# Stick-breaking attention: scores from high and low parts, and the projections that feed them one half-step earlier

## What is computed

```python
def stick_breaking_attention(h, w_qkv, w_o):
    qkv = (h @ w_qkv).reshape(b, s, 3, SB_HEADS, HEAD_DIM)
    q, k, v = qkv[:, :, 0], qkv[:, :, 1], qkv[:, :, 2]
    ...
        z = jnp.einsum('bqhd,bshd->bhqs', q_blk, k).astype(jnp.float32) * scale
        causal = key_pos[None, :] < t[:, None]
        log_1m = jnp.where(causal, jax.nn.log_sigmoid(-z), 0.0)
        excl = lax.cumsum(log_1m, axis=3, reverse=True) - log_1m
        a = jnp.where(causal, jnp.exp(jax.nn.log_sigmoid(z) + excl), 0.0)
        return jnp.einsum('bhqs,bshd->bqhd', a.astype(v.dtype), v)
```

## Times and profile before

| | us |
|---|---|
| median of 3 runs | 2158.74 |
| lowest, highest | 2157.59, 2158.87 |
| the profiled execution, device time | 2157.02 |
| its span, first to last instruction | 2155.2 |

### The profile page before, as it was taken

How to read it: one execution, slowest core, us unless ns; L and a number is a source line. 1 busy time by engine, 2 the same in 40 slices (tenths; PEclk the granted TensorE clock), 3 DMA queues, 4 the chain that set the end, 5 groups by cost and what they waited for, 6 DMA issues and landing times.

```text
span 2155.2 us, 32285 instructions
## 1 busy us (share of the span) xinstructions
PE 2120.9 (98%) x12608; PEld 1768.3 (82%) x12608; DVE 1536.7 (71%) x2132; ACT 1002.8 (47%) x1690; POOL 727.5 (34%) x604
## 2 busy tenths in 40 slices
PE   8999999999999999999999999999999999999998
PEld 6888788888999998766688999988965568898987
DVE  5866566557988876387759787776567756777774
ACT  4433464345544444465554333344536755343434
POOL 2300330017434434074554332311146636332321
PEclk9999999999999999999999999999999999999999
DMA  5233125313333333311133333233420012323231
GB/s 178 83 108 88 50 78 159 86 57 91 99 109 108 112 94 98 88 40 50 40 88 99 99 98 118 85 112 101 142 66 2 1 40 79 118 88 108 93 104 49
DMA packets 293303, 188.77 MB, mean 88 GB/s; under 512 B 8224, under 2 KB 287008, under 8 KB 293152
## 3 DMA queue, kind: packets, MB, share of 16 engines
q1 hardware_dynamic: 292864, 186.51, 28.9%
q10 hardware_dynamic: 288, 0.21, 0.0%
HBM read 183.81 MB, written 2.10 MB: 86 GB/s over the span
## 4 chain that ended last, share of the span: by engine, by line
PE 89%; DVE 5%; ACT 3%; issue 2%; POOL 0%; DMA 0%; ACTq 0%; DVEq 0%; POOLq 0%
PE ps L539 87%; PE ps L573 2%; DVE wl L512 1%; ACT wh L502 1%; DVE sb_small L3228 1%; DVE H L682 0%; DVE tmp L1169 0%; ACT XH L560 0%; ACT sq L616 0%; DVE ns_x L3268 0%; DVE ns_x L3267 0%; ACT p_xscr L722 0%; DVE nt_pts L3251 0%; DMA p_xt<-in_x 0%; ACT tp_tb L1894 0%
## 5 line engine op out<-in xcount | busy, mean ns | idle before, releaser
L512 DVE TENSOR_TENSOR wl<-raw,wh 128x1024 fp32r<-128x1024 f32 (+1 forms) x336 | 433.1, 1302 | 239.7 <-ACT wh L502 239.2
L539 PE MATMUL ps<-xb_x,wh 128*128 128x256 f32 (+1 forms) x1584 | 388.6, 336 | 2.2 <-DVE wl L512 1.0
L502 ACT CAST wh<-raw 128x1024 fp32r<-128x1024 f32 (+1 forms) x336 | 324.3, 980 | 132.6 <-PE ps L539 123.8
L539 PEld LDWEIGHTS ps<-xb_x,wh 128*128 128x128 f32 x1584 | 265.2, 188 | 32.1 <-ACT tp_q L2104 0.9
L539 PE MATMUL ps<-tt_t,wh 128*128 128x256 f32 x1536 | 277.5, 280 | 2.0 <-ACT tp_q L2100 2.0
L539 PE MATMUL ps<-xb_x,wl 128*128 128x256 f32 (+1 forms) x792 | 264.8, 334 | 0.0
L539 PEld LDWEIGHTS ps<-tt_t,wh 128*128 128x128 f32 x1536 | 237.1, 188 | 5.8 <-ACT tp_q L2100 2.9
L539 PE MATMUL ps<-XH,wh 128*128 128x512 f32 (+2 forms) x632 | 234.5, 371 | 4.9 <-issue 4.0
L539 PE MATMUL ps<-XH,wl 128*128 128x512 f32 (+2 forms) x632 | 229.8, 364 | 0.0
L539 PE MATMUL ps<-XL,wh 128*128 128x512 f32 (+2 forms) x632 | 229.4, 363 | 0.0
L539 PE MATMUL ps<-tt_t,wl 128*128 128x256 f32 x768 | 214.2, 279 | 0.0
(11 more groups left out here) (429 smaller groups left out, 4669.9 us busy)
## 6 DMA issues: line engine op xcount, KB each, us to landing
raw<-in_mlp_w SPq DMA_DIRECT2D x128, 512.0 KB, 4.0
raw<-in_w_gate_up SPq DMA_DIRECT2D x44, 512.0 KB, 3.9
raw<-in_w_in SPq DMA_DIRECT2D x29, 512.0 KB, 3.7
raw<-in_sb_w_qkv SPq DMA_DIRECT2D x24, 512.0 KB, 3.6
raw<-in_w_down SPq DMA_DIRECT2D x22, 512.0 KB, 5.9
raw<-in_w_out_mix SPq DMA_DIRECT2D x16, 512.0 KB, 3.5
raw<-in_w_kv SPq DMA_DIRECT2D x16, 512.0 KB, 3.7
raw<-in_nsa_w_kv SPq DMA_DIRECT2D x12, 512.0 KB, 3.6
```

The lines of the kernel that those rows point to most:

```text
L502: e.copy(shaped(WH[i % NH], i), source(i)).then_inc(*w_hi.up(i))
L512: e.tensor_tensor(shaped(WL[i % NH], i), source(i), shaped(WH[i % NH], i).bitcast(F), ALU.subtract).then_inc(*w_lo.up(i))
L539: return e.matmul(out, a, b, start=start, stop=stop, skip_group_check=True)
```

## The change

Queries and keys are now split. `dve_stick_qk` evicts a projection in float32 into one of two `tmp` buffers instead of into `q_s` or `k_s`. A new ACT cast, `act_stick_qk`, writes the high part (fp32r) to `q_s` or `k_s`. A new DVE subtraction, `dve_stick_qk_lo`, writes the low part to one of four buffers (`qk_lo`, tiles `sl_a`, `sl_b`, `sl_c`). `pe_stick_scores` makes three fp32r products for each head (high by high, low queries, low keys), first for both heads, then the next, and waits for the low parts. `next_qk` is one step ahead of what it was, so that the loops run from n = -2: a projection is made in steps (0,1), (2,3), ... instead of (1,2), (3,4), ...; its eviction and both new steps stand in even n, the weight cast on ACT in even n and the weight subtraction on DVE in odd n (before: odd and even).

```diff
--- before.py
+++ after.py
@@ -2272,12 +2272,16 @@
 
 
     ph = Phase(XAT, "st")
-    q_s = ph.sb("q", [128, 8, S])
-    k_s = ph.sb("k", [128, 8, S])
+    q_s = ph.sb("q", [128, 8, S], R)
+    k_s = ph.sb("k", [128, 8, S], R)
     XO = Pair(*(Phase(XAT + 4 * 8 * S * i, f"so{i}").sb("x", [128, 8, S], R) for i in range(2)))
     ph = Phase(PH0 + 32768, "st")
     v_s = ph.sb("v", [128, 4, D])
     rs1 = Phase(PH0 + 92160, "st").sb("rs1", [128, S])
+    phl = Phase(PH0 + 94208, "sl")
+    qk_lo = [[Phase(PH0 + 90112, "sl").sb("a", [128, S], R), phl.sb("b", [128, S], R)],
+             [phl.sb(f"c{i}", [128, S], R) for i in range(2)]]
+    qk_low = [[Buf(t) for t in pair] for pair in qk_lo]
     wd = [512 - 128 * j for j in range(4)]
     wl_ = [512, 384, 384, 128]
     ST = [(c, j) for c in range(8) for j in (3, 2, 1, 0)]
@@ -2311,26 +2315,43 @@
 
     def next_qk(n):
 
-        u, half = (n + 1) // 2 + 2, (n + 1) % 2
+        u, half = (n + 2) // 2 + 2, n % 2
         return (u if u < 16 else None), half
+
+    def left_qk(n):
+
+        u, half = next_qk(n - 1)
+        return QK[u] if half and u is not None and n > -2 else None
 
     OUT_AT = {NST - 2: [(0, 0, 2)], NST - 1: [(0, 2, 6)], NST: [(0, 6, 7), (1, 0, 2)], NST + 1: [(1, 2, 6)],
               NST + 2: [(1, 6, 7)]}
     OUT_LAST = [(2, 0, 3), (0, 7, 8), (1, 7, 8), (2, 3, 8)]
 
     def plan_stick():
+        def plan_qk(o, bank):
+            plan(bank, ("sqk", o), (v_made, ("sqk", o)))
+
+        def plan_parts(u):
+            o = QK[u]
+            plan(tmp.bufs[2 + u % 2], ("qkt", o), (x_lo, ("qk", o)))
+            plan(qk_low[o % 8 % 2][o // 8], ("qkl", o), (scored, ("z", 4 * (o % 8) + 3, 1)))
+
         for o in QK[0:2]:
-            plan(psr.next(), ("sqk", o), (v_made, ("sqk", o)))
+            plan_qk(o, psr.next())
         for blk in range(2):
             token_plan(f"sv{blk}", 4)
             if blk == 0:
                 plan_spread("st")
+        for u in range(2):
+            plan_parts(u)
         plan_spread("one")
+        for u in range(2, 16):
+            plan_parts(u)
         pairs = Ring([0, 1, 2])
-        for n in range(-1, NST):
+        for n in range(-2, NST):
             u, half = next_qk(n)
             if u is not None and half == 0:
-                plan(NB, ("sqk", QK[u]), (v_made, ("sqk", QK[u])))
+                plan_qk(QK[u], NB)
             if n < 0:
                 continue
             c, j = ST[n]
@@ -2392,12 +2413,15 @@
     def pe_stick_scores(e, n):
 
         c, j = ST[n]
-        e.wait_ge(*v_made.at("sqk", c))
-        e.wait_ge(*v_made.at("sqk", 8 + c))
+        e.wait_ge(*x_lo.at("qk", c))
+        e.wait_ge(*x_lo.at("qk", 8 + c))
         bk = [take(e, ("sk", n, m))[:, 0:wd[j]] for m in range(2)]
-        for m in range(2):
-            p0 = 64 * m
-            mm(e, bk[m], k_s[p0:p0 + 64, c, 128 * j:128 * j + 128], q_s[p0:p0 + 64, c, 128 * j:512], True, False)
+        ql, kl = got(("qkl", c)), got(("qkl", 8 + c))
+        for k, q, first in ((k_s[:, c, :], q_s[:, c, :], True), (k_s[:, c, :], ql, False),
+                            (kl, q_s[:, c, :], False)):
+            for m in range(2):
+                p = slice(64 * m, 64 * m + 64)
+                mm(e, bk[m], k[p, 128 * j:128 * j + 128], q[p, 128 * j:512], first, False)
         for m in range(2):
             mm(e, bk[m][:, 0:128], Ib[:, :], maskb[:, 2, :], False, False).then_inc(*scored.up("z", n, m))
 
@@ -2460,6 +2484,7 @@
             pe_tokens(e, f"sv{blk}", [f"sv{blk}{c}" for c in range(4)], XB, "st", 512, 4, 2,
                       between={0: pe_sum, 2: pe_spread} if blk == 0 else {})
         pe_spread(e, "one")
+        pe_stick_qk(e, -2)
         pe_stick_qk(e, -1)
         for n in range(NST + 3):
             if n < NST:
@@ -2479,6 +2504,10 @@
             project(e, f"so{o}", XO, "so", t[:, :], ("soo", o))
         pe_.end("st")
 
+    def act_stick_qk(e, o):
+        e.wait_ge(*v_made.at("sqk", o))
+        e.copy((k_s if o >= 8 else q_s)[:, o % 8, :], got(("qkt", o))[:, :]).then_inc(*x_hi.up("qk", o))
+
     def act_stick(e):
         act_weights(e, UI["sv02"])
         fence(e, "f")
@@ -2494,6 +2523,9 @@
                 act_weights(e, UI[f"sv{blk}{c}"] + 2)
                 if blk == 0 and c == 2:
                     act_rs(e, "st", [(v_made, ("f", ff.last_up))])
+                if blk == 0 and c == 3:
+                    for o in QK[0:2]:
+                        act_stick_qk(e, o)
             if blk == 0:
                 e.wait_ge(*v_made.at("inv", "st"))
             act_tokens(e, f"sv{blk}", lambda t: v_s[:, t, 512 * blk:512 * blk + 512], 512, 4, inv("st"))
@@ -2509,7 +2541,7 @@
                 e.wait_ge(*scored.at("cum" if m else "cum0", n))
                 e.activation(L[:, m, 0:wd[j]], got(("sk", n, m))[:, 0:wd[j]], ACT.Exp).then_inc(*a_made.up("sw", n, m))
 
-        for n in range(-1, NST + 3):
+        for n in range(-2, NST + 3):
             if 2 <= n < NST + 2:
                 weights_of(n - 2)
             u, half = next_qk(n)
@@ -2517,6 +2549,8 @@
                 act_weights(e, UI[f"sq{QK[u]}"] + 2)
             if n == NST - 2:
                 act_weights(e, UI["so2"])
+            if left_qk(n) is not None:
+                act_stick_qk(e, left_qk(n))
             if 0 <= n < NST:
                 c, j = ST[n]
                 L = got(("L", n))
@@ -2603,14 +2637,19 @@
         e.tensor_scalar(sum_parts(n)[0], f[:, :, :], 1.0, 0.0, ALU.mult, ALU.add).then_inc(*g_made.up("hi_sum", n))
 
     def dve_stick_qk(e, o):
-        b, t = o % 8, got(("sqk", o))
+        d, t = take(e, ("qkt", o)), got(("sqk", o))
         e.wait_ge(*proj.at("sqk", o))
         e.wait_ge(*a_made.at("rs", "st"))
         if o < 8:
-            f = e.scalar_tensor_tensor(q_s[:, b, :], t[:, :], 0.125, rs[:, :], ALU.mult, ALU.mult)
+            f = e.scalar_tensor_tensor(d[:, :], t[:, :], 0.125, rs[:, :], ALU.mult, ALU.mult)
         else:
-            f = e.tensor_tensor(k_s[:, b, :], t[:, :], rs[:, :], ALU.mult)
+            f = e.tensor_tensor(d[:, :], t[:, :], rs[:, :], ALU.mult)
         f.then_inc(*v_made.up("sqk", o))
+
+    def dve_stick_qk_lo(e, o):
+        d, hi = take(e, ("qkl", o)), (k_s if o >= 8 else q_s)[:, o % 8, :]
+        e.wait_ge(*x_hi.at("qk", o))
+        e.tensor_tensor(d[:, :], got(("qkt", o))[:, :], hi.bitcast(F), ALU.subtract).then_inc(*x_lo.up("qk", o))
 
     def dve_stick(e):
         dve_weights(e, UI["sv02"])
@@ -2633,19 +2672,24 @@
                 if blk == 0 and c == 2:
                     for o in QK[0:2]:
                         dve_stick_qk(e, o)
+                if blk == 1 and c == 0:
+                    for o in QK[0:2]:
+                        dve_stick_qk_lo(e, o)
         dve_diag(e, "one")
-        for n in range(-1, NST + 3):
+        for n in range(-2, NST + 3):
             u, half = next_qk(n)
             if u is not None and half:
                 dve_weights(e, UI[f"sq{QK[u]}"] + 2)
             if n == NST - 2:
                 dve_weights(e, UI["so2"])
-            if half == 0 and 2 < (n + 1) // 2 + 2 <= 16:
-                dve_stick_qk(e, QK[(n + 1) // 2 + 1])
+            if left_qk(n) is not None:
+                dve_stick_qk(e, left_qk(n))
             if 0 <= n < NST:
                 dve_stick_abs(e, n)
             if 1 <= n < NST + 1:
                 dve_stick_lo(e, n - 1)
+            if left_qk(n) is not None:
+                dve_stick_qk_lo(e, left_qk(n))
             if 0 <= n < NST:
                 dve_stick_terms(e, n)
             if 1 <= n < NST + 1 and ST[n - 1][1] in (1, 2):
```

## The result

| | before | after |
|---|---|---|
| median, runs side by side | 2157.42 (2157.12 to 2158.87, 6 runs) | 2170.49 (2168.19 to 2172.07, 6 runs) |
| the profiled execution's span | 2155.2 | 2169.9 |

A forecast was written before the change was run, and what follows sets the result against it. It took PE to bound the loop up to step 25 and the other engines' chain after; scores -2.3, late evictions +6.55 and step 26's lost half projection +1.4 gave +5.65 us, 2164.4, range 2158.2 to 2168.2.

The follow-up runs named there:

- e6: Kernel before, with only the second half of the last projection made on PE in step 25, leaving none in step 26: 2159.86 us, ratio 1.0011.
- e2: Changed kernel with the projections back where they were before, so only the split with its casts, subtractions and three products: 2164.16 us, ratio 1.003.
- e7: Changed kernel with projections where they were before, and the keys' eviction, cast and subtraction placed earlier on DVE and ACT: 2157.07 us, ratio 0.9999.
- e8: e7 with DVE's weight subtraction of steps 0, 4, 8, ... put behind `dve_stick_lo`: 2156.32 us, ratio 0.9995.
- e10: Changed kernel with DVE's weight subtraction in even steps, the 512-wide sum behind the eviction, and nine output products moved to step 27: 2159.58 us.
- e11: Changed kernel with the work on H (ACT's scaling, POOL's product) in steps 13 to 20 instead of 4 to 11: 2170.77 us.

## What to carry to other kernels

When a change moves work on an engine with an unbroken row up to a deadline, add up the whole row with each instruction at its length beside its neighbour's, and take the end of the bounds that the nearest row speaks for; every instruction that need not stand ahead of the deadline goes behind it. Do this sum for the first, shorter cycles too. If a stage is bound by one engine in its body and by a chain in its tail, work pulled ahead of the body is paid in full, and what comes back in the tail has to be shown: here it was 0.5 to 1.1 of 2.75 us, and nothing with the tail alone.

## What the runs showed of the hardware

A wait of PE shown as 1.49 us cost 1.76. At the end of the loop PE's granted clock fell behind short waits (0.57 in six us of e6, behind waits of 0.67 and 1.49; 0.63 in six us of e2, behind a single one of 2.76). It did so in the traces of all kernels here but before, e7 and e8. These three wait 1.2 to 1.4 us in all in steps 26 to 30; those with a fall there waited 1.8 to 2.8 (e10: 1.2, and then 2.57 in step 31). Waits of 1.5 to 1.9 once every 24 us mostly had no such fall behind them: of the twelve in steps 4 to 24 of the two traces of after, one had, and none of the six in e11.
